# Grouped-query attention: context tiles of a head pair as one unit, placed between the image groups

## What is computed

```python
def gqa_attention(q, k, v):
    scale = HEAD_DIM ** -0.5
    def block(j, qb):
        logits = jnp.einsum("bqhgd,bkhd->bhgqk", qb, k).astype(jnp.float32) * scale
        p = jax.nn.softmax(logits, axis=-1).astype(v.dtype)
        return jnp.einsum("bhgqk,bkhd->bqhgd", p, v)
    return map_query_blocks(block, q)
...
    o = gqa_attention(q, jnp.concatenate([kc, k], axis=1),
                      jnp.concatenate([vc, v], axis=1)).reshape(b, s, MIX_WIDTH)
    oc = gqa_attention(qc, kc, vc).reshape(b, n_ctx, MIX_WIDTH) if need_ctx else None
```

## Time and profile before

| | |
|---|---|
| median of 3 runs | 3018.88 us (3017.0 to 3021.44) |
| profiled execution, own time | 3015.66 us |
| its span, first to last instruction | 3013.8 us |
| granted TensorE clock, mean | 0.978 |
| busy: TensorE, VectorE, ScalarE, GpSimd | 93%, 51%, 32%, 26% |
| the stage in question | 1101.5 to 1323.4 us, 221.9 us |
| of it TensorE busy | 207.6 us |

### The profile page before, as it was taken

The page is one execution under the profiler, slowest core; times in us unless marked ns, Lnnn a source line. Parts: engine busy times, 40 slices in busy tenths (PEclk is TensorE's granted clock), DMA queues, the critical chain, the costliest instruction groups (busy, mean ns, idle before and its releaser), DMA issues. The chain is left out here.

```text
span 3013.8 us, 57209 instructions
## 1 busy us (share of the span) xinstructions
PE 2808.9 (93%) x23728; PEld 2072.0 (69%) x23728; DVE 1543.4 (51%) x2764; ACT 960.3 (32%) x2236; POOL 769.2 (26%) x969
## 2 busy tenths in 40 slices
PE   6989998999998989999999989999998898999999
PEld 4968788775645877754788857547887575468674
DVE  5655765744326745422652356239823773265552
ACT  2022322214421235532111257221212673212660
POOL 3312313210024500012322124135521422253000
PEclk9999999999999999999999989999999999999999
DMA  6230100103321121112101261021112120212000
GB/s 232 81 116 19 41 17 3 46 33 109 128 107 35 56 98 57 57 57 99 56 33 62 71 231 28 15 90 56 57 56 99 61 80 29 98 62 109 18 1 28
DMA packets 108034, 205.91 MB, mean 68 GB/s; under 512 B 21795, under 2 KB 25394, under 8 KB 107264
## 3 DMA queue, kind: packets, MB, share of 16 engines
q1 hardware_dynamic: 107504, 201.36, 19.1%
q0 software_dynamic: 272, 0.89, 0.1%
HBM read 186.91 MB, written 15.54 MB: 67 GB/s over the span
## 5 line engine op out<-in xcount | busy, mean ns | idle before, releaser
L665 PE MATMUL psum<-weights,h_t 128*128 128x256 f32 x1488 | 352.0, 379 | 1.0 <-ACT p_u_u L749 1.0
L665 PEld LDWEIGHTS psum<-weights,h_t 128*128 128x128 f32 x1488 | 279.6, 190 | 38.6 <-ACT p_u_u L749 1.4
L1299 DVE TENSOR_REDUCE neg_max<-psum 128x1 f32<-128x768 f32 (+1 forms) x192 | 159.9, 865 | 221.6 <-PE psum L1169 176.0
L665 PE MATMUL psum<-z_l,x_tiles 128*128 128x256 f32 x816 | 192.8, 379 | 0.0
L665 PEld LDWEIGHTS psum<-z_l,x_tiles 128*128 128x128 f32 x816 | 155.0, 190 | 21.1
L1862 PE MATMUL psum<-weights,q_l 128*128 128x512 f32 x384 | 166.5, 592 | 0.0
L760 ACT ACTIVATE square<-psum 128x512 f32<-128x512 f32 (+1 forms) x80 | 45.0, 565 | 377.4 <-DVE psum L1017 242.9
L1190 PE MATMUL psum<-eye,prob 128*128 128x128 f32 x832 | 136.2, 287 | 11.3 <-DVE prob_t L1317 3.9
L1346 POOL TENSOR_TENSOR z_l<-z_l,inv_total 128x128 f32<-128x128 f32 x80 | 32.1, 401 | 429.7 <-DVE inv_total L1310 429.7
L1264 ACT ACTIVATE prob<-psum,neg_max 128x768 f32<-128x768 f32 (+1 forms) x160 | 129.7, 817 | 21.4 <-DVE neg_max L1299 15.1
L1862 PEld LDWEIGHTS psum<-weights,q_l 128*128 128x128 f32 x384 | 72.2, 190 | 87.1 <-issue 87.1
(11 more groups left out here) (440 smaller groups left out, 6055.8 us busy)
## 6 DMA issues: line engine op xcount, KB each, us to landing
weights<-in_ada_w_dram SPq DMA_DIRECT2D x30, 2048.0 KB, 8.0
weights<-in_a_w_in_dram SPq DMA_DIRECT2D x10, 2048.0 KB, 8.6
weights<-in_b_w_in_dram SPq DMA_DIRECT2D x8, 2048.0 KB, 7.9
weights<-in_c_w_in_dram SPq DMA_DIRECT2D x8, 2048.0 KB, 7.8
weights<-in_w_in_dram SPq DMA_DIRECT2D x6, 2048.0 KB, 8.2
x_aside<-x_tiles SPq DMA_DIRECT2D x24, 512.0 KB, 2.6
x_tiles<-x_aside SPq DMA_DIRECT2D x4, 3072.0 KB, 12.7
weights<-in_a_w_out_dram SPq DMA_DIRECT2D x4, 2048.0 KB, 7.8
```

What stands on the lines that cost most here:

```text
L665: last = pe.matmul(dst, lhs[:, k, :], rhs[k // 2][:, k % 2, :], start=k == 0, stop=k == KH - 1)
L1299: last = dve.tensor_reduce(neg_max[:, i % 4, m:m + 1], score(i, m, 0, keys), AX, ALU.max, negate=True)
```

## The change

Each head pair's two context tiles become one unit ("joined" = 2). Its scores are 256 columns for each tile and head, side by side in the head's slot, 512 in all. One VectorE instruction takes the maxima of both tiles, ScalarE makes one exponential for each tile (two per head), all eight transposes make two fills, ordered so that the blocks of both tiles of one key tile and head lie side by side, and each matmul of the mix has 256 columns. The first fill is copied by ScalarE and the second by VectorE: the rule is now that VectorE copies the last fill of a unit that has more than one, which for image units is what it was. GpSimd scales the z of both tiles.

The order of the units changes too: for each head pair first the joined context unit, a group of its own, then the four image units. That makes 8 x 5 = 40 units. `mod_rows_at` is computed from the new n, and the row sums then stand at units 5, 13, 19, 24, 30 and 35. With joined = 1 (latent attention, last layer) the same instructions come out as before, in the same order.

The diff, cut to its core:

```diff
-        for u, tile in enumerate(pair["tiles"]):
-            units.append(dict(group=len(groups), col=u, last=u == len(pair["tiles"]) - 1, **tile))
-        groups.append(dict(dst=pair["dst"], last=len(units) - 1, z=[t["z"] for t in pair["tiles"]]))
+        tiles, joined = pair["tiles"], pair["joined"]
+        for u in range(0, len(tiles), joined):
+            units.append(dict(group=len(groups), col=u, last=u + joined == len(tiles), rows=tiles[u]["rows"],
+                              keys=tiles[u]["keys"], k=tiles[u]["k"], v=tiles[u]["v"], joined=joined,
+                              q=[t["q"] for t in tiles[u:u + joined]], z=[t["z"] for t in tiles[u:u + joined]]))
+        groups.append(dict(dst=pair["dst"], last=len(units) - 1, z=[t["z"] for t in tiles]))
...
     mod_rows_at = {}
     for c in range(6 if next_mod else 0):
         at = (c + 1) * n // 7
-        mod_rows_at[at - 1 if units[at]["last"] else at] = c
+        while units[at]["last"]:
+            at -= 1
+        mod_rows_at[at] = c
...
+    def transposed(i):
+
+        return 2 * units[i]["joined"] * (units[i]["keys"] // P)
+
+    def part_of(i, kt):
+
+        return 2 * units[i]["joined"] * kt // 4
+
     def parts(i):
 
-        return -(-2 * (units[i]["keys"] // P) // 4)
+        return -(-transposed(i) // 4)
...
-                    for a in range(0, keys, 256):
-                        for m in range(2):
-                            last = pe.matmul(score(i, m, a, a + 256), units[i]["q"][m], units[i]["k"][m][:, a:a + 256],
-                                             start=True, stop=True)
-                            if a + 256 == keys:
-                                last.then_inc(*scored.tick())
+                    for t, q in enumerate(units[i]["q"]):
+                        for a in range(0, keys, 256):
+                            to = keys * t + a
+                            for m in range(2):
+                                last = pe.matmul(score(i, m, to, to + 256), q[m], units[i]["k"][m][:, a:a + 256],
+                                                 start=True, stop=True)
+                                if to + 256 == keys * units[i]["joined"]:
+                                    last.then_inc(*scored.tick())
...
-                    kt, m = x // 2, x % 2
+                    km, t = divmod(x, units[i]["joined"])
+                    kt, m = divmod(km, 2)
+                    at = units[i]["keys"] * t + P * kt
                     last = pe.transpose(TURN[:, P * (x - cols.start):P * (x - cols.start) + P],
-                                        prob[:, i % 3, m, P * kt:P * kt + P], pr.eye[:, :])
+                                        prob[:, i % 3, m, at:at + P], pr.eye[:, :])
...
+                t = units[i]["joined"]
                 for kt in range(first, until):
-                    if kt == first or kt % 2 == 0:
-                        pe.wait_ge(*emptied.at(fills["probs", i, kt // 2]))
+                    if kt == first or part_of(i, kt) > part_of(i, kt - 1):
+                        pe.wait_ge(*emptied.at(fills["probs", i, part_of(i, kt)]))
                     for m in range(2):
-                        last = pe.matmul(OUT[64 * m:64 * m + 64, P * col:P * col + P], units[i]["v"][m][kt],
-                                         prob_t[:, i % 2, 2 * kt + m, :], start=(kt == 0), stop=(kt == kts - 1))
...
+                        x = t * (2 * kt + m)
+                        last = pe.matmul(OUT[64 * m:64 * m + 64, P * col:P * (col + t)], units[i]["v"][m][kt],
+                                         prob_t[:, i % 2, x:x + t, :], start=(kt == 0), stop=(kt == kts - 1))
...
-                act.activation(prob[:, i % 3, m, 0:keys], score(i, m, 0, keys), ACT.Exp, bias=neg_max[:, i % 4, m:m + 1],
-                               accum_out=total[:, i % 4, m:m + 1]).then_inc(*exped.tick())
+                for t in range(units[i]["joined"]):
+                    last = act.activation(prob[:, i % 3, m, keys * t:keys * t + keys], score(i, m, keys * t, keys * t + keys),
+                                          ACT.Exp, bias=neg_max[:, i % 4, m, t:t + 1],
+                                          accum_out=total[:, i % 4, t, m:m + 1])
+                last.then_inc(*exped.tick())
...
-                for g in range(min(parts(i), 2) if here else 0):
+                for g in range((2 if parts(i) > 2 else 1) if here else 0):
...
-                last = dve.tensor_reduce(neg_max[:, i % 4, m:m + 1], score(i, m, 0, keys), AX, ALU.max, negate=True)
+                scores = score(i, m, 0, keys * t).rearrange("p (t k) -> p t k", t=t)
+                last = dve.tensor_reduce(neg_max[:, i % 4, m, 0:t], scores, AX, ALU.max, negate=True)
...
-                if 0 <= i < n and parts(i) > 2:
-                    take_turned(i, 2)
+                if 0 <= i < n and parts(i) > 1:
+                    take_turned(i, parts(i) - 1)
...
+                for t, z in enumerate(units[i]["z"]):
+                    heads = z.rearrange("p (m f) -> p m f", m=2)
+                    last = pool.tensor_tensor(heads, heads, wide(inv[:, i % 4, t, :], 2, 64), ALU.mult)
+                last.then_inc(*scaled.tick())
...
-    for queries in [range(XT)] + ([range(XT, NT)] if ctx_out else []):
-        keys = range(NT) if queries[0] < XT else range(XT, NT)
-        kc = slice(P * keys[0], P * (keys[-1] + 1))
-        for j in range(8):
-            g = j // 2
+    for j in range(8):
+        g = j // 2
+        for queries in ([range(XT, NT)] if ctx_out else []) + [range(XT)]:
+            keys = range(NT) if queries[0] < XT else range(XT, NT)
+            kc = slice(P * keys[0], P * (keys[-1] + 1))
...
-            pairs.append(dict(tiles=tiles, dst=q_t[:, j, P * queries[0]:P * (queries[-1] + 1)]))
+            pairs.append(dict(tiles=tiles, joined=2 if queries[0] >= XT else 1,
+                              dst=q_t[:, j, P * queries[0]:P * (queries[-1] + 1)]))
```

More of the change, by code:

```diff
@@ L1127, in pair_attention_stage @@
         gate_t = local("gate_t", [P, SEQ])
-        neg_max = local("neg_max", [P, 4, 2])
-        total = local("total", [P, 4, 2])
-        inv = local("inv_total", [P, 4, 2])
+        neg_max = local("neg_max", [P, 4, 2, 2])
+        total = local("total", [P, 4, 2, 2])
+        inv = local("inv_total", [P, 4, 2, 2])
         if next_mod:
@@ L1149, in turned @@
         def turned(i, g):
-            return slice(4 * g, min(4 * g + 4, 2 * (units[i]["keys"] // P)))
+            return slice(4 * g, min(4 * g + 4, transposed(i)))
         @block.tensor
@@ L1176, in do_score @@
                             b = min(a + 512, keys)
-                            last = pe.matmul(score(i, m, a, b), units[i]["q"][m], units[i]["k"][m][:, a:b],
+                            last = pe.matmul(score(i, m, a, b), units[i]["q"][0][m], units[i]["k"][m][:, a:b],
                                              start=True, stop=True)
@@ L1296, in do_max @@
             def do_max(i, m):
-                keys = units[i]["keys"]
+                keys, t = units[i]["keys"], units[i]["joined"]
                 dve.wait_ge(*scored.at(2 * i + m + 1))
-                last = dve.tensor_reduce(neg_max[:, i % 4, m:m + 1], score(i, m, 0, keys), AX, ALU.max, negate=True)
+                scores = score(i, m, 0, keys * t).rearrange("p (t k) -> p t k", t=t)
+                last = dve.tensor_reduce(neg_max[:, i % 4, m, 0:t], scores, AX, ALU.max, negate=True)
                 if i in rows_at:
@@ L1309, in do_inverse @@
                     dve.wait_ge(*scaled.at(i - 3))
-                dve.reciprocal(inv[:, i % 4, :], total[:, i % 4, :]).then_inc(*summed.tick())
+                t = units[i]["joined"]
+                dve.reciprocal(inv[:, i % 4, 0:t, :], total[:, i % 4, 0:t, :]).then_inc(*summed.tick())
             def take_turned(i, g):
@@ L3182, in mla_branch @@
                           z=latent["z"][t][:, P * j:P * j + P]) for t in range(XT)]
-            pairs.append(dict(tiles=tiles, dst=mix_t[:, PAIRS + j, :]))
+            pairs.append(dict(tiles=tiles, joined=1, dst=mix_t[:, PAIRS + j, :]))
         pair_attention_stage(pr, pairs, next_mod=True, spare=kept)
```

2 lines of the change are left out of this document (removed).

## The result

The changed kernel takes 3033.41 us (median of 6 runs, 3028.55 to 3043.56), the kernel before in the same comparison 3017.94 us (6 runs). The ratio is 1.005, with a 95% interval of 1.0034 to 1.0067. The forecast was 3033 with a range of 3022 to 3040, and slower. The number was right.

The account below looks back on a forecast made before the run. TensorE, busy 93% of the span, with VectorE nearly level in image steps. Terms -41.0 + 5.8 + 44.5 + 5.0 = +14.3 us on the profiled 3015.66 give 3030; with 3.2 to the median, 3033, range 3022 to 3040.

Parts of the forecast that it names:

- context tail: Stage end after the last image score: 55.91 us becomes 14.88, as in the last layer's stage, so -41.0 us.
- row sums and columns brought back: Two row sums at 2.3 us and the columns at 1.2, formerly in the removed stretch, come back: +5.8 us.
- first joined unit, in the start: Stage start at half clock: shorter first score, a wait for GpSimd, one step more; together +5.0 us.
- seven cycles above 20.36: Each later cycle of four image units and a joined unit takes 26.71 us against 20.36: +44.5 us in all.
- The new wait: ScalarE's gate copy waits for the previous image group's finish, delaying exponential and score: 1.37 us of stall per cycle.
- Step C: Step transposing the joined unit: its missing fill gains nothing, 4.97 us, and the new wait makes it 6.34.
- Step I0: Step transposing a group's first image unit: 5.10 us, as ScalarE is behind and its copies come late.
- I2: Step transposing the third image unit, scoring the joined one: 4.55 us, plus 0.48 for the image group's gate.
- I3: Step transposing the fourth image unit: a full image step, 4.97 us, plus 0.3 for the joined unit's gate transposes.
- Rival 3: Clock falls in each of seven cycles behind two close gaps, 2 to 3 us each: +28 to +35, chance 0.04.
- Rivals 1 and 2: Rival 1: the new wait does not stall, sum +3.8 us, 3022.7, chance 0.09; rival 2 has its own line.
- rival 2: Interleaving pays: TensorE's own work sets the pace, 3.80 us per joined unit, sum -4.8, 3014 us; chance 0.04.

Follow-up runs that it names:

- two_gates: Changed kernel with two gate buffers, ScalarE's gate copy waiting only for the group before the last one: 3026.62 us, ratio 1.002 to the kernel before.
- one_gate_act: Changed kernel with its one gate buffer, but ScalarE copies both fills of a joined unit: 3030.08 us, ratio 1.0037 to the kernel before.
- before_two_gates: Control: the kernel before with two gate buffers: 3015.65 us, ratio 0.9973.
- changed_again: The changed kernel run once more, unedited: 3039.15 us, ratio 1.0062 to the kernel before.
- changed_third: The changed kernel a third time, unedited, for the clock: one run, 3041.46 us.
- two_gates_act: Changed kernel with two gate buffers, and ScalarE copies both fills of a joined unit: 3017.43 us, ratio 0.999 to the kernel before.
- join_end_gates_act: Changed kernel with joined units in a row at the end, two gate buffers, ScalarE copying both fills: 3017.43 us, ratio 0.9994 to the kernel before.
- behind_only: Changed kernel with each joined unit behind the four image units of its head pair: 3028.26 us, ratio 1.0029 to the kernel before.
- between_only: Changed kernel without joining: two single context units as a group ahead of each image group: 3033.82 us, ratio 1.0044 to the kernel before.
- join_only: Changed kernel with image groups first and the eight joined units in a row at the end: 3025.48 us, ratio 1.0017 to the kernel before.

## Why the prediction was right, step by step

| term | forecast | measured (first profile) |
|---|---|---|
| context tail, last score to end: 55.91 to | 14.88 | 14.89 |
| row sums and columns brought back | +5.8 | +4.8 (what remains) |
| first joined unit, in the start | +5.0 | 22.07 - 14.19 = +7.9 |
| seven cycles above 20.36 | 7 x 6.35 = +44.5 | 7 x 5.79 = +40.5 |
| stage | +14.3 | +12.2 |

- *The tail and the drain* were taken from the last layer's stage and came out to 0.01 us. A piece of the trace that already has the form which the change brings is the best source of a price.
- *The new wait* was named with its place, its chain and its count: it is there seven times, and taking it away gives back 1.28 us a cycle against 1.37 forecast. This is the mechanism that carries the sum, and it is shown by two_gates, with one_gate_act for the chain and before_two_gates as the control.
- *Step C gains nothing from its missing fill*: right in kind. Its size was off. I let VectorE's copy start at +3.58, as in the image step. There, the copy doesn't wait for VectorE alone: the copy had waited for the third fill's transposes. Two rows of the timeline of the kernel before that I had not weighed, from the image step of the earlier trace rows:

```profile
1265.40 0.66 PE L1190 MATMUL psum<-eye,prob 128*128 128x128 f32 x4
...
1265.99 0.88 PE L1203 MATMUL psum<-prob_t,v_l 128*64 128x128 f32 x12
```

They run until 1265.40 + 0.66 = 1266.06, and the copy follows at 1266.10. The product at 1266.91 has a like reason: the second half of the mix ends at 1265.99 + 0.88 = 1266.87. In step C both are ready earlier. The copy starts at 1198.34 - 1194.93 = +3.41, so the transposes start at +4.22 instead of +4.42, the product at +3.99 instead of +4.39, the score at +6.07 instead of +6.34. Step I0 took 4.93 instead of 5.10, with VectorE's copy at 1204.53 - 1201.00 = +3.53: the backlog of ScalarE that I had added doesn't show there. These two steps make 0.44 of the 0.56 us between 26.71 and 26.15; most of the rest is in I2 and I3 with their gate transposes (4.99 and 5.20 instead of 5.03 and 5.27). The error of method is one: I read a start from a row and took it for the engine's own limit, without asking what had ended last ahead of it.
- *The start* was priced at +5.0 with +-1.4 for one stretch at half clock; it cost 7.9, outside these bounds. Two more scores at half clock than before are 2.7 us. The later stretch has a cause that I could have named, the same copy standing behind two maxima while TensorE had nothing else to do (wait of 2.08 us). one_gate_act shows it: the earlier copy takes 2.5 us off the start. changed_again and changed_third show that the length repeats (in changed_third the clock was at half before the wait already).
- *Row sums*: 2.35 us each where they stand at an image unit, 1.9 at a joined unit, whose step has slack for them (28.04 us between the group ends at 1255.92 and 1283.96). I had 2.3 for all. That is why less came back than the 5.8: three of the six now stand at joined units, and the columns took 1.4 (29.45 - 26.15 - 1.9).
- *Maxima of two tiles* took 0.687 us each, as taken. No effect, as said. Two of them merge to a row of 1.29 us, since one starts before the other has ended; the view by lines and forms of after, 1156 to 1320 us, gives the mean of one:

```profile
L1322 DVE TENSOR_REDUCE neg_max<-psum 128x2 f32<-128x512 f32 x12 | 7.9, 687 | 14.9 <-PE psum L1184 14.9
```

- *Rival 3, the clock,* had 0.04 and came in part: in none, two and four of seven cycles, at 1.34 to 1.64 us each, not 2 to 3 us in all seven. The prediction called itself wrong if the clock in the stage was under 1.00 after its start. By that sign it held in the first profile and failed in the other two; I had treated the clock as all or nothing, and it is neither.
- *The step to the median* was luck. The profiled execution came out at 3028.55 us against 3030 (a cycle cheaper than forecast, -4.0; a dearer start, +2.9; row sums, -1.0; and 0.8 us in other stages). The median lies 4.9 us above it; I had added 3.2, from three runs of the kernel before. Falls of the clock in this stage are not enough to explain the spread of the changed kernel's runs over 15 us: the profile of changed_again is 10.5 us longer than the first one, of which 2.7 lie in this stage, and changed_third 12.9, of which 5.9. The kernel before spreads over 20 us as well in one of its comparisons.
- *Rivals 1 and 2* are out for the changed kernel: the stall exists, and without it the change is still 0.2% slower. But rival 2 had its conditions right. Where both are met (two_gates_act: the copy out of VectorE's list, the gate copy not waiting) a joined unit cost 3.87 us where the rival had 3.80, and the stage came out 3.8 us shorter where it had 4.8. What gained there was the joining: without the waits the stage is 217.7 us joined in a row, 218.1 joined between images and 216.3 with each joined unit behind its images, so interleaving as such gave 1.4 us at best. The Trainium skill, page "Perfetto Trace Analysis", section Optimization Strategy, says that interleaving regimes may improve a kernel in which the most-contended engine changes over time. I had left that condition out when I let the section speak for the change and expect the side of rival 2 (the "third case" of that passage, counted with the forecast as the first). By the trace it isn't met: TensorE was the busiest engine in both parts, 148.14 of 152.00 us in the image part (1120 to 1272 us) and 45.67 of 51.40 in the context part. Placing alone made the stage 16.3 us longer (238.2 against 221.9), though only 5.7 us of gaps stood in the context part. Another sentence of the same section fits this trace: that a gap which repeats can mean too few buffers for the next tile. It names SBUF and PSUM space; here the buffer that was short was gate_t, of which there was one, and with a second the gap of 1.22 us was gone from all seven cycles.

Put in costs per head pair (context, without row sums): a pair of units in a row 4.57; joined in a row 5.17; joined between images 5.79; single between images 6.7; joined without the two waits 4.00 in a row and 3.87 between images. Joining did save TensorE some time (busy 3.74 us per joined unit in join_end_gates_act, 4.10 in the pair's 4.57 us), and the change lost more than that in two waits which the new form itself brings.

## What to carry to other kernels

When a group of work shrinks to one step, look at each single buffer that is handed on from group to group: what was released a step early is now released in the same step, by the engine's last instruction. Price a step from the row in which the engine in question is the last to arrive, and check in the row before it what it had waited for. And after removing work from one engine in a step where two are level, write down what the other still has in front of its first instruction that anybody waits for.

## What the runs showed of the hardware

In the changed form TensorE has two gaps, of 0.61 and 1.22 us within 2.5 us, in every cycle of 26 us or more. Behind them the granted clock fell from 2.4 to 1.2 GHz in none, two and four of seven cycles in three profiles of the same program, and in three cycles of behind_only; it cost 1.34 to 1.64 us each time in the changed kernel. A gap of 1.55 us in each cycle was followed by no fall in the one profile that has it, and neither were the pairs of gaps in between_only (1.17 and 1.15 us) and join_only (0.41 and 0.94 us). Why it falls in some cycles and not in others stays open: the three profiles are of the same instructions, though not all of the same chip.

The control shows how far a total may be trusted here: an edit without effect on its stage (221.6 against 221.9 us) came out 0.27% faster, beyond its own interval.
